# Second attention's gate and output kept turned, indexer scores in pairs, half of the mixer split on GpSimd, another order of steps

## The reference

```
h    = rmsnorm(x, norm_w);  proj = h @ w_in         # 4 x 512 (A), 4 x 512 (B), 4*64+64+4 (indexer)
A:   ao = softmax(q1 k1 + bias) v - lam * softmax(q2 k2 + bias) v      # 4 heads of 128
     ao = rmsnorm(ao, subln_w) * (1 - lambda_init) * silu(ag)
B:   score[q,k] = sum_h iw[q,h] * relu(iq[q,h] . ik[k])                # 4 heads of 64
     keep the 256 best keys of each query; softmax(q k + bias) v over these   # 8 heads of 64
     bo = bo * silu(bg)
y    = concat(ao, bo) @ w_out;  out = rmsnorm(x + y, final_norm_w)
```

## Time and profile before

| | |
|---|---|
| median of 3 runs | 753.26 us (752.53 to 753.86) |
| the profiled execution's own time | 754.53 us |
| its span, first to last instruction | 752.7 us |
| TensorE busy | 97% of the span |
| VectorE, GpSimd, ScalarE busy | 80%, 46%, 43% |
| indexer scores alone | 58.0 to 71.4 us |
| group A projected | 71.4 to 245.6 us |
| first attention | 245.6 to 372 us |
| group B projected | 372 to 525 us |
| second attention | 525 to 653.6 us |
| output | 653.6 to 752.7 us |

### The profile page before, as it was taken

One profiled execution on the slowest core, in us unless ns is written; L12 is line 12 of the kernel. 1 busy time (PEld: TensorE's weight loads), 2 busy tenths in 40 slices (PEclk: granted clock), 3 DMA queues, 4 the chain that ended last, 5 costly groups with the idle time before them and its releaser, 6 DMA issues.

```text
span 752.7 us, 12086 instructions
## 1 busy us (share of the span) xinstructions
PE 730.8 (97%) x4216; PEld 607.5 (81%) x4216; DVE 603.2 (80%) x1301; ACT 325.7 (43%) x731; POOL 348.1 (46%) x429
## 2 busy tenths in 40 slices
PE   8999999999999999999999999999899989999996
PEld 7756888888888798999888888888777878788886
DVE  5548999999999979888599999996777767545444
ACT  7447122131313666667531131316766766523222
POOL 5220222222646869771236565548999996300000
PEclk9999999999999999999999999999999999999999
DMA  7331112121230010113021211220021022313131
GB/s 276 106 110 56 42 44 56 42 57 43 53 88 1 0 43 2 43 30 99 15 71 43 56 43 42 56 70 11 20 57 45 15 57 85 100 56 112 57 113 56
DMA packets 24564, 44.58 MB, mean 59 GB/s; under 512 B 3076, under 2 KB 10936, under 8 KB 24376
## 3 DMA queue, kind: packets, MB, share of 16 engines
q1 hardware_dynamic: 23352, 42.76, 19.3%
q10 hardware_dynamic: 1152, 1.05, 0.4%
HBM read 35.40 MB, written 6.57 MB: 56 GB/s over the span
## 4 chain that ended last, share of the span: by engine, by line
PE 61%; DVE 22%; POOL 12%; issue 3%; ACT 1%; POOLq 0%; ACTq 0%; DVEq 0%
PE psum L1252 23%; PE psum L1475 12%; DVE score L1661 10%; DVE top L1656 9%; PE psum L1347 4%; PE psum L1335 3%; PE psum L1172 3%; PE psum L1313 3%; PE psum L1144 3%; PE psum L1190 2%; PE psum L1316 2%; POOL near_low L747 2%; PE psum L1364 2%; POOL k_high_twice L608 1%; POOL near_high L747 1%
## 5 line engine op out<-in xcount | busy, mean ns | idle before, releaser
L604 POOL TENSOR_TENSOR w_lo<-w_raw,w_hi 128x512 fp32r<-128x512 f32 x60 | 77.8, 1299 | 220.0 <-ACT w_hi L788 219.7
L1661 DVE MATCH_REPLACE8 score<-top,score 128x768 f32<-128x768 f32 (+5 forms) x176 | 157.3, 906 | 0.0
L1656 DVE MAX8 top<-score 128x8 f32<-128x768 f32 (+5 forms) x176 | 148.2, 909 | 1.0
L788 ACT ACTIVATE w_hi<-w_raw 128x512 fp32r<-128x512 f32 x60 | 37.6, 630 | 211.9 <-PE psum L1252 208.9
L964 ACT ACTIVATE probs<-psum,small 128x384 f32<-128x384 f32 (+7 forms) x128 | 94.7, 742 | 47.9 <-DVE small L1682 29.9
L1252 PE MATMUL psum<-w_hi,big_hi 128*128 128x512 f32 x256 | 99.6, 389 | 0.0
L1252 PE MATMUL psum<-w_lo,big_hi 128*128 128x512 f32 x256 | 99.6, 389 | 0.0
L1252 PE MATMUL psum<-w_hi,big_lo 128*128 128x512 f32 x256 | 99.6, 389 | 0.0
L1252 PE MATMUL psum<-big_hi,w_hi 128*128 128x512 f32 x192 | 74.8, 390 | 0.0
L1252 PE MATMUL psum<-big_hi,w_lo 128*128 128x512 f32 x192 | 74.7, 389 | 0.0
L1252 PE MATMUL psum<-big_lo,w_hi 128*128 128x512 f32 x192 | 74.7, 389 | 0.0
(11 more groups left out here) (193 smaller groups left out, 1619.2 us busy)
## 6 DMA issues: line engine op xcount, KB each, us to landing
w_raw<-in_w_in SPq DMA_DIRECT2D x62, 256.0 KB, 2.7
xs<-in_x SPq DMA_DIRECT2D x8, 512.0 KB, 6.8
k_high_twice<-k_high_twice SPq DMA_DIRECT2D x16, 256.0 KB, 3.7
xres<-in_x SPq DMA_DIRECT2D x8, 512.0 KB, 4.3
out_y<-y_out SPq DMA_DIRECT2D x8, 384.0 KB, 2.9
w_tail<-in_w_out SPq DMA_DIRECT2D x10, 256.0 KB, 2.6
bias_scratch<-bias_row SPq DMA_DIRECT2D x1, 2304.0 KB
bias<-bias_scratch SPq DMA_DIRECT2D x12, 128.0 KB, 2.9
```

The lines of the kernel that those rows point to most:

```text
L604: pool.tensor_tensor(lo[:, 0:cols], w_staged(n)[:, 0:cols], hi[:, 0:cols].bitcast(f32), ALU.subtract).then_inc(w_lo_made, 1)
L788: act.activation(w_parts(n)[0][:, 0:cols], w_staged(n)[:, 0:cols], ACT.Copy).then_inc(w_hi_made, 1)
L1656: ins = dve.max(top8[:, i - SEL0, :], sc)
L1661: ins = dve.match_replace(sc, top8[:, i - SEL0, :], sc, TAKEN)
```

## The change

- **Start.** norm_w's small DMA moves from SP's queue to ScalarE's. ScalarE scales x tiles 6 and 7, VectorE no longer tile 6. VectorE's `variance(6)` and `norm(6)` come earlier.
- **Indexer.** The first six `score_idx` come as three pairs of adjacent instructions. Four relu buffers instead of two. VectorE does four rounds of `select` on tile 2 before `move_iwT(1)`.
- **Selection.** The last of tile 7's rounds moves from before the first attention to the very end, and VectorE makes tile 7's mask itself, after that (`last_mask_made`).
- **Second attention.** The gate group is projected turned ("T"), so `mixB` holds head dimension by query. `weigh_heads` gives the output in this form already, so it isn't turned back. Instead the reciprocal sums are spread over 128x128 (`share`), turned by TensorE (`turn_shares`), and multiplied into the gate (`scale_gate`); `finishB` multiplies the output from PSUM into it. The order of tiles is 4, 0, 5, 1, 6, 3, 7, 2 instead of 5, 0, 4, 1, 6, 2, 7, 3. On TensorE the turns of a long step (more than four key blocks) are spread between the next step's scores; on ScalarE a short step's `turned` stands between two exponentials. VectorE moves the second group of a short step instead of the first.
- **GpSimd.** w_out's chunks come at other steps (`OUT_TIMES`); SP's loads follow.
- **Output.** `turn_mix`, `mix_high` and `mix_low` handle `mixA` alone. GpSimd splits `mixB` straight into the high and low parts (`mixB_parts`), and TensorE waits for it (`mixBT_split`) at the fifth of eight blocks.

```diff
-        ORDER = ([2, 4, 6, 7, 5, 3, 1, 0], [5, 0, 4, 1, 6, 2, 7, 3])
+        ORDER = ([2, 4, 6, 7, 5, 3, 1, 0], [4, 0, 5, 1, 6, 3, 7, 2])
...
-        short = {quads[1, s][0][0] for s in range(STEPS) if len(quads[1, s]) == 2}
+        short = {quads[1, s][1][0] for s in range(STEPS) if len(quads[1, s]) == 2}
...
+        OUT_TIMES = [(0, 4), (1, 4), (1, 6), (2, 4), (2, 6)] + [(3, piece) for piece in range(7)]
...
# GpSimd, second attention
-                elif b < 3 and piece == 4:
-                    w_out_parts(CHUNKS + 2 * b)
-                    w_out_parts(CHUNKS + 2 * b + 1)
-                    wait_split(pool, CHUNKS + 2 * b + 1)
-                elif b == 3 and piece < 6:
-                    w_out_parts(CHUNKS + 6 + piece)
-                    wait_split(pool, CHUNKS + 6 + piece)
+                elif (b, piece) in OUT_TIMES:
+                    n = CHUNKS + OUT_TIMES.index((b, piece))
+                    w_out_parts(n)
+                    wait_split(pool, n)
             pool.wait_ge(s_ready, 4 * STEPS)
+            def mixB_parts(t):
+                hi, lo = mx_hi[:, t % 2, BLOCKS:DB, :], mx_lo[:, t % 2, BLOCKS:DB, :]
+                src = mixB[:, :, t * P:(t + 1) * P]
+                pool.wait_ge(o_moved, STEPS + last_step(t) + 1)
+                if t >= 2:
+                    pool.wait_ge(y_ready, 2 * t - 2)
+                link(pool.tensor_scalar(hi, src, 1.0, 0.0, ALU.mult, ALU.add))
+                pool.tensor_tensor(lo, src, hi.bitcast(f32), ALU.subtract).then_inc(mixBT_split, 1)
+            mixB_parts(0)
             for n in range(LATE, CHUNKS + 2 * DB):
                 w_out_parts(n)
+            for t in range(1, TILES):
+                mixB_parts(t)
...
# ScalarE
-                if n >= 2:
-                    act.wait_ge(idx_added, n - 1)
+                if n >= RELUS:
+                    act.wait_ge(idx_added, n - RELUS + 1)
...
# TensorE
             for n in range(3):
-                score_idx(n)
+                score_idx(2 * n)
+                score_idx(2 * n + 1)
                 project_idx(1, n + 2)
                 turn_late(n + 5)
-            for n in range(3, 6):
-                score_idx(n)
-                project_idx(1, n + 2)
+            for d in range(5, DB):
+                project_idx(1, d)
...
-                if j == 0 and s == 0:
-                    pe.wait_ge(o_moved, STEPS)
-                elif j == 0:
-                    pe.wait_ge(o_out, s)
+                if j == 0:
+                    pe.wait_ge(o_moved, STEPS + s)
...
+            def turn_shares(s):
+                pe.wait_ge(shares_made, s + 1)
+                pe.wait_ge(gate_scaled, s)
+                pe.transpose(bank(BACK_BANK)[:, 0:P], shares.rearrange("p m d -> p (m d)"), ident[:, :]
+                             ).then_inc(shares_turned, 1)
...
# VectorE
-            select(FIRST, done=(SEL0,))
-            select(1, TILES - 2)
+            select(FIRST - FIRST_EARLY, done=(SEL0,))
+            select(FIRST_EARLY, SEL0 + 1)
+            select(1, TILES - 2, TILES - 1)
...
             select(1, SEL0 + 1, TILES - 2, done=range(SEL0 + 1, TILES - 2))
-            def move_out(s):
-                dve.wait_ge(pv_done, quads_through(1, s))
-                dve.tensor_copy(oT[:, :], bank(O_BANK)[:, 0:P]).then_inc(o_out, 1)
+            select(1, TILES - 1)
+            last_score = score[:, score_off[TILES - 1]:score_off[TILES - 1] + SEQ]
+            dve.tensor_scalar(mask[:, score_off[TILES - 1]:score_off[TILES - 1] + SEQ], last_score, TAKEN, MASKED,
+                              ALU.not_equal, ALU.mult).then_inc(last_mask_made, 1)
+            def share(s):
+                c = 2 * s % 8
+                dve.wait_ge(dve_own, inverted[1, s])
+                if s >= 1:
+                    dve.wait_ge(shares_turned, s)
+                dve.tensor_copy(shares[:, :, :], rinv[:, c:c + 2].unsqueeze(2).broadcast_to([P, 2, HEAD])
+                                ).then_inc(shares_made, 1)
+            def scale_gate(s):
+                b, i = place_of(1, s)
+                g = mixB[:, b, i * P:(i + 1) * P]
+                dve.wait_ge(shares_turned, s + 1)
+                dve.tensor_tensor(g, bank(BACK_BANK)[:, 0:P], g, ALU.mult).then_inc(gate_scaled, 1)
             def finishB(s):
...
+                dve.tensor_tensor(g, bank(O_BANK)[:, 0:P], g, ALU.mult).then_inc(o_moved, 1)
...
             for s in range(STEPS + 2):
                 qs = quads[1, s - 1] if 1 <= s <= STEPS else []
+                if 1 <= s <= STEPS:
+                    invert(1, s - 1)
+                    share(s - 1)
                 if s >= 2:
-                    move_out(s - 2)
+                    finishB(s - 2)
                 turned(1, qs)
                 if s + 1 < STEPS:
                     for m in range(2):
                         far_min(1, s + 1, m)
                         soften(1, s + 1, m)
-                if s >= 2:
-                    invert(1, s - 2)
-                    finishB(s - 2)
+                if 1 <= s <= STEPS:
+                    scale_gate(s - 1)
```

211 lines of the change are left out of this document (103 added, 108 removed).

## The result

The changed kernel takes 741.7 us in the median of four runs (741.52 to 744.05), the kernel before, beside it, 753.12 us: 11.4 us less, a ratio of 0.9855 with a 95% interval from 0.9834 to 0.9877. The forecast was 742.7 us in a range from 737.5 to 748.5. The profiled execution has a span of 739.8 us against 752.7, 12.9 less, and the same difference in its own time, 741.63 against 754.53; that of before had run 1.4 us above the 753.12, that of after at its median. What follows splits up the 12.9 us.

What follows compares the result with a forecast made beforehand. TensorE bounds the kernel, with VectorE and GpSimd deciding in places, chiefly at the second attention's block borders. Terms 0.5 + 2.7 + 0.5 + (2.9 + 0.8 - 0.3) + 0.9 + 2.6 = 10.6 us off 753.26 give 742.7 us, range 737.5 to 748.5.

Steps and rivals of the forecast that it cites:

- pairs: Indexer: three pairs instead of six single early scores, heads running side by side on TensorE, save 2.7 us.
- relu buffers: Indexer: with four buffers ScalarE runs ahead of VectorE's additions; 0.5 us taken, between nothing and 1 us.
- four early rounds: Indexer: VectorE's four selection rounds on tile 2, 4.4 us, fit idle time; if late, 0.5 us at worst.
- second attention with two halves of turn_mix: Second attention: 2.9 us from GpSimd, 0.8 clock, 0.3 lost to orders, 0.9 from fewer transposes for tiles 0 and 1.
- rival C: Indexer: score pairs don't overlap at 384 columns, only the third saves; 1.7 us back, 744.4 us; 6% chance.
- GpSimd's order: Second attention's block borders: one w_out chunk fewer before VectorE's near tile; TensorE saves 2.9 us, then waits for keys.
- that sign: At the second attention's block borders, VectorE waits for no near tile and TensorE waits for keys instead.
- Clock: Second attention, block 3: the clock's fall, 1.6 us if it goes; half booked, 0.8 us.
- Orders: Second attention: 0.6 us lost to VectorE's longer stretch, 0.3 us gained by the shorter last step.
- VectorE: Second attention: net +0.2 us a step, 1.6 a block, against 7.8 us idle; 0.6 us loss booked.
- Rival D: Second attention: each copy into `shares` waits for GpSimd, over 1.21 us needed; slower kernel, 756 us; 4% chance.
- Rival A: Second attention: a full queue still paces it, only work taken from TensorE counts; 7.2 us, 746.1 us; 25% chance.

Runs made afterwards that it cites:

- w_out places: Changed kernel with GpSimd's w_out chunks at their old places: 744.77 us. The kernel before with only the new places: 750.37 us.
- four more transposes: Changed kernel with four more transposes of mixA, into a bank nothing reads, in each output tile from the third on: 744.89 us.
- transposes ahead: Changed kernel with the second attention's opening idle transposes (14, not 10) ahead of the second step's first scores: 741.17 us.
- keys first: Changed kernel with GpSimd splitting keys before queries in second-attention blocks 1 to 3, idle transposes moved ahead, three early selection rounds: 740.79 us.

## Why the prediction was right, and where it was not

The total was 11.4 us against my 10.6 by the medians, 12.9 by the traces. Term by term, by the trace:

| step | forecast | trace | shown by |
|---|---|---|---|
| start | 0.5 | 0.4 | first pair at 33.57 us, one score at 33.95 before |
| pairs | 2.7 | 3.1 | single scores |
| relu buffers | 0.5 | 2.2 | two buffers |
| four early rounds | 0 | -0.6 | waits for ikT and iw; three rounds |
| second attention with two halves of turn_mix | 4.3 | 5.0 | w_out places (2.8), the rest below |
| output | 2.6 | 2.7 | four more transposes |

(Rounded; the traced terms add up to 12.8.) That the total came so near is in part luck: the relu buffers gave 1.7 us more than I booked, and the early rounds took 0.6 that I had at nothing. The 4.3 us of the second attention hold 0.8 us for the clock that no run can place, and 0.3 us for the orders.

*Start and pairs.* Right, and rival C is out. TensorE's wait of 0.56 us for VectorE's tile 6 is gone, and one of 0.28 us for `big_lo` stands shortly before its place; no run takes the parts of the start apart.

*Relu buffers: the term that failed.* "I take 0.5" was a size read from a single wait. The upper bound, 1 us, was too low as well: it was 2.2. With two buffers ScalarE waits for VectorE's additions all along the stretch, and 56 matmuls take 13.44 us that take 11.24 with four.

*Early rounds.* I had written that the copy of ikT would hold n = 8 for "0.5 us at worst"; it was 1.01 us. With the wait for iw behind it, the fourth round costs 0.6 us and not all of the 1.01, for without it ScalarE's relu is next in line. The sum "4 x (0.56 + 0.54) = 4.4 us" left out that a third instruction stands between the two of a round: the four rounds took 4.96 us (45.85 to 50.81). They were not late by much, and one fewer removes the wait.

*Selection.* Right: the late mask and round of tile 7 hold nothing, and the time between the indexer and the second attention is unchanged.

*GpSimd's order.* "Each border has one chunk fewer ahead of the near tile" was right in mechanism and size: 2.8 us of the stage when undone, 2.8 alone, forecast 2.9. That "the keys decide" then was right for TensorE: 0.87 us at block 3, 2.20 to 2.72 in three other executions of the same code. But in those three VectorE still waits 1.07 to 1.58 us for a near tile there; only in the changed kernel's own execution and in the one with three early rounds (0.86 us for the keys) does it wait for none. So that sign held at blocks 1 and 2, and at block 3 in two executions of five.

*Clock.* The 0.8 us did not come as I put it. The fall left block 3 but appeared in the first stretch, behind TensorE's 1.68 us of waiting. There it cost nothing, because GpSimd sets the pace behind it: with the clock whole the stage is as long. At block 3 a fall cost 2.0 us in the one pair of executions that differ by it, where I had 1.6. What its absence there gave the changed kernel, no run shows.

*Orders.* I booked 0.3 us. Undone in the traces, the order of tiles costs 1.0 us of the stage, mostly as waits for keys, and the order of turns 0.4; neither is shown by the runs. With 2.8 for the places of the chunks and 0.9 for turn_mix's halves they would make 5.1 of the 5.0 us.

*VectorE.* I charged 0.6 us for its longer stretch. `shares` took 662 ns in the mean, not the 400 I took from the earlier trace rows; VectorE's blocks are 25.4 and 26.9 us instead of 24.6. TensorE waited for it four times, 1.6 us in all, never over 0.5, and never for finishB. What the longer stretch cost, no run shows. Rival D needed 1.21 us of wait on every step; the copy's excess over its least was 1.1 at most and 0.4 in the mean.

*Rival A* had the truest picture of the stage: a full GpSimd queue. It did not decide the total, since the chunk at each border was indeed the late piece, but it is what the next gain had to remove. I had argued against it that "TensorE's long waits lie at borders alone"; so they do, and here the borders are where the full queue shows.

*Output.* Right. From one tile to the next it is now 11.37 us, where it was 11.79, from the 664.95 of the earlier trace rows to the next such row, and no wait of TensorE for GpSimd's halves shows. The chain, before and then in the changed kernel:
```profile
676.74 0.87 PE psum L1387 x8
```
```profile
655.02 10.93 PE psum L1494 x48
...
666.39 10.93 PE psum L1494 x48
```

Left open: why the clock's fall sits in the first stretch in one execution, behind a wait of 1.68 us, and at block 3 or nowhere in others that have the same wait at the same place.

## What to carry to other kernels

Where one engine is fed by a second engine's long in-order queue, the waits can show at the borders of stages alone, as here. Before reordering what is late there, see whether the queue has any idle time between the borders. Here it had none, and two repairs (transposes ahead, keys first) only changed the name of the wait; what paid was to take work out of the queue there and put it where it was idle. The sign of such a pacemaker was the length of the stage, the same to 0.4 us in six executions with quite different waits; the busy share was 93% with and without it. Size a buffer count from the whole stretch, not from one wait. Behind each wait that you remove, look for the next engine in line before you book its length.

## What the runs showed of the hardware

VectorE's write of `shares` within SBUF lasts until just behind the GpSimd instruction that runs when it starts. Timelines of VectorE and GpSimd in the changed kernel:
```profile
594.78 1.34 DVE L1817 COPY shares<-small 128x128 f32<-128x128 f32 x1
```
```profile
594.77 1.27 POOL L616 TENSOR_TENSOR kT_r<-kT,k_high_twice 64x512 fp32r<-64x512 f32 x1
```
GpSimd's instruction ends at 596.04, VectorE's at 596.12. In 26 of the 32 copies the end lies 0.07 to 0.10 us behind the end of a GpSimd instruction that ran when the copy started (583.89 + 1.22 = 585.11 behind 585.03 is another); in five GpSimd is in a row of near tiles whose single ends the timeline merges, and with GpSimd idle, at 633.10, the copy took 0.23 us, near the least of 226 ns. This agrees with what the Trainium skill ("SBUF — State Buffer", section "Who interferes with whom") says of a one-source copy in a two-port mode: it and GpSimd lock each other out for a whole instruction. That this copy, whose source is broadcast, runs in such a mode is inferred from its waits. The two-source form waits in the same way (1349 ns at 595.05, behind a GpSimd instruction that ends at 596.25; its ends lie 0.13 to 0.15 us behind). VectorE's products that read one operand from PSUM never took over 293 ns beside the same GpSimd (278 to 293 and 276 to 293 ns, 32 each).

It goes the other way too. In the output, VectorE and GpSimd:
```profile
655.35 0.69 DVE L1890 TENSOR_TENSOR y_out<-y,fw 128x512 f32<-128x512 f32 x1
656.10 1.10 DVE L1905 SCALAR_TENSOR_TENSOR small<-small 128x1 f32<-128x1 f32 x1
```
```profile
655.45 1.74 POOL L787 TENSOR_TENSOR mx_lo<-mixB,mx_hi 128x512 fp32r<-128x512 f32 x1
```
GpSimd's subtraction, 1.28 us for the tile before (at 645.17), began behind VectorE's two-source product and took 1.74; and VectorE's one-column product then ended with it, 656.10 + 1.10 = 657.20 against 657.19. TensorE waited for none of these.
